# Experts' rows and results transposed on VectorE in 32x32 blocks over quarter rows, in place of TensorE transposes

## The reference

```python
def _clamped_swiglu(u):
    glu, lin = jnp.split(u, 2, axis=-1)
    glu = jnp.minimum(glu, SWIGLU_LIMIT)
    lin = jnp.clip(lin, -SWIGLU_LIMIT, SWIGLU_LIMIT)
    return glu * jax.nn.sigmoid(SWIGLU_ALPHA * glu) * (lin + 1.0)

def expert_block(args):                      # 128 tokens of one expert
    xb, e = args
    u = xb @ w_in[e] + b_in[e]               # 1024 -> 2048, the "up" product
    return _clamped_swiglu(u) @ w_out[e] + b_out[e]   # 1024 -> 1024, the "down" product

x = x + g_f[:, None] * _moe(h, ...)          # sum over a token's experts, weighted by its gates
return _rmsnorm(x, final_norm_g)
```

## Time and profile before

| | |
|---|---|
| median of 3 runs | 1981.47 us (1980.3 to 1984.21) |
| span of the profiled execution, first to last instruction | 1959.1 us |
| TensorE busy | 1923.4 us, 98% of the span |
| VectorE busy | 655.1 us, 33% |
| ScalarE busy | 467.9 us, 24% |
| GpSimd busy | 217.5 us, 11% |
| granted TensorE clock, mean | 0.997 of full speed |
| DRAM traffic, mean over the span | 265 GB/s |

### The profile page before, as it was taken

How to read it: one execution, slowest core, us unless ns; L and a number is a source line. 1 busy time by engine, 2 the same in 40 slices (tenths; PEclk the granted TensorE clock), 3 DMA queues, 4 the chain that set the end, 5 groups by cost and what they waited for, 6 DMA issues and landing times.

```text
span 1959.1 us, 50916 instructions
## 1 busy us (share of the span) xinstructions
PE 1923.4 (98%) x22971; PEld 1732.3 (88%) x22971; DVE 655.1 (33%) x1890; ACT 467.9 (24%) x1382; POOL 217.5 (11%) x250
## 2 busy tenths in 40 slices
PE   7999999999999999999999999999999999999997
PEld 4756765566999999999999999999999999999997
DVE  2655766665331212121222222222222222222224
ACT  3104544441121111111111112121211111122213
POOL 2003000001010101020201011101011110110002
PEclk9999999999999999999999999999999999999999
DMA  9880121116988888887969796969697988999986
GB/s 360 307 181 20 44 76 54 44 54 207 363 316 295 292 323 311 298 309 278 333 255 354 263 355 252 371 245 369 245 380 253 370 319 327 340 330 337 323 320 223
DMA packets 150208, 523.95 MB, mean 267 GB/s; under 512 B 10027, under 2 KB 15811, under 8 KB 149987
## 3 DMA queue, kind: packets, MB, share of 16 engines
q1 hardware_dynamic: 131186, 467.68, 65.7%
q0 software_dynamic: 17200, 52.59, 7.9%
q10 hardware_dynamic: 1600, 0.36, 0.1%
HBM read 485.34 MB, written 34.21 MB: 265 GB/s over the span
## 4 chain that ended last, share of the span: by engine, by line
PE 94%; DVE 2%; SPq 1%; DMA 1%; issue 1%; ACT 0%; POOL 0%; ACTq 0%; DVEq 0%; POOLq 0%
PE ps L1683 47%; PE ps L1721 24%; PE ps L1518 5%; PE ps L1466 4%; PE ps L1526 3%; PE ps L1671 2%; PE ps L1644 2%; PE ps L1444 2%; PE ps L1498 1%; PE ps L1462 1%; DMA ring<-in_w_qkv 1%; PE ps L1487 1%; SPq L416 0%; SPq L428 0%; PE ps L1415 0%
## 5 line engine op out<-in xcount | busy, mean ns | idle before, releaser
L1683 PE MATMUL ps<-U,ring 128*64 128x120 f32 (+11 forms) x13312 | 935.5, 270 | 1.7 <-issue 1.7
L1683 PEld LDWEIGHTS ps<-U,ring 128*64 128x64 f32 (+1 forms) x13312 | 923.1, 149 | 9.5 <-issue 7.9
L1721 PE MATMUL ps<-U,ring 128*64 128x120 f32 (+11 forms) x6656 | 468.4, 270 | 0.1
L1721 PEld LDWEIGHTS ps<-U,ring 128*64 128x64 f32 (+1 forms) x6656 | 461.4, 149 | 4.1 <-issue 3.4
L1253 DVE TENSOR_SCALAR U<-ps,U 128x120 f32<-128x120 f32 (+11 forms) x256 | 90.7, 354 | 1089.6 <-PE ps L1683 1089.6
L829 ACT ACTIVATE U<-U 128x120 f32<-128x120 f32 (+11 forms) x256 | 80.2, 313 | 889.7 <-DVE U L1253 889.7
L840 ACT ACTIVATE U<-ps,U,modT 128x120 f32<-128x120 f32 (+11 forms) x256 | 119.0, 465 | 286.8 <-PE ps L1721 286.7
L593 POOL DMA_INDIRECT acc_d<-U x43 | 43.2, 1005 | 849.5 <-DVE U L1245 845.8
L1518 PE MATMUL ps<-ring 128*128 128x512 f32 (+1 forms) x288 | 114.9, 552 | 0.0
L1518 PEld LDWEIGHTS ps<-ring 128*128 128x128 f32 x288 | 53.4, 190 | 54.4 <-issue 52.9
L815 ACT ACTIVATE U<-ps,modT,Af 128x120 f32<-128x120 f32 (+11 forms) x252 | 91.9, 469 | 9.2 <-PE ps L1656 9.2
(11 more groups left out here) (231 smaller groups left out, 1100.3 us busy)
## 6 DMA issues: line engine op xcount, KB each, us to landing
ring<-in_moe_w SPq DMA_DIRECT2D x191, 2048.0 KB, 11.1
U<-in_w_mod SPq DMA_DIRECT2D x8, 2048.0 KB, 12.2
ring<-in_w_mod SPq DMA_DIRECT2D x3, 2048.0 KB, 19.4
ring<-in_w_qkv SPq DMA_DIRECT2D x3, 2048.0 KB, 18.5
acc_d<-xr SPq DMA_DIRECT2D x10, 512.0 KB, 3.4
xr<-in_x SPq DMA_DIRECT2D x8, 512.0 KB, 9.5
ring<-in_w_o SPq DMA_DIRECT2D x2, 2048.0 KB, 8.6
xn_d<-U SPq DMA_DIRECT2D x8, 512.0 KB, 2.6
```

Source lines behind the costliest of these rows:

```text
L1683: last = pe.matmul(bank(j % 4)[lo:hi, s * 256:s * 256 + n], w[:, k, s, (j % 2) * P + lo:(j % 2) * P + hi], xT[:, k, 0:n], start=(k == 0), ...
L1721: last = pe.matmul(bank(m % 4)[lo:hi, 0:n], w[:, k, (m % 4) * P + lo:(m % 4) * P + hi], actT[:, k, 0:n], start=(k == 0), stop=(k == KT - 1))
```

## The change

- A row of 1024 features is treated as four **quarter rows** of 256. 32 tokens times 4 quarters fill 128 partitions, which is called a **turn**; a slot of width n takes ceil(n/32) turns (3 to 6; 143 over all slots). GpSimd gathers and scatters quarter rows of 1 KB by index tables (`xq_rows`, `yq_rows`), one indirect DMA for each turn, and gates one number for each quarter row.
- VectorE turns 32x32 blocks: a partition quarter then holds 32 features of its quarter row. `rows_turn(r + 1)` stands behind slot r's last activation, two instructions; `rows_back(r - 1)`, two instructions and one multiply-add for each turn, stands behind the evacuation of up product 3 (wide slot) or 5 (narrow), or 1 in the last slot.
- So that the blocks fit the products, the host lays out the weights, the norm's gain and the modulation in another order of features (`into_experts`, `out_of_experts`, `by_piece`). Input features are taken with a stride of 8 elements (`features`), in the router's transposes too.
- ScalarE scales the turned rows from SBUF to SBUF in place (`rows_scale`) instead of reading PSUM.
- Down products go to banks 4 to 7, so that they wait neither for an up product's evacuation nor up products for a down product's. Their eight K steps stand one behind the other as before.
- The index tables need a product and some VectorE instructions, placed in slot 0 (`places_by_row`, `places_product`, `places_by_quarter`).
- The first slot's rows and the last slot's results are still turned on TensorE.

```diff
+        def features(rows, k):
+            return rows.rearrange("p (n k) -> p k n", k=KT)[:, k]
...
         def back_behind(r):
-            return 4 if wide(r - 1) and not wide(r) else 0
+            return 0 if r == LAST_SLOT else 2 if wide(r) else 4
...
+            def gather_quarters(r):
+                for v in range(turns(r)):
+                    pool.indirect_dma_start(out=xq[:, v, :], out_offset=None, in_=xn_q,
+                                            in_offset=bass.IndirectOffsetOnAxis(ap=xq_rows[:, v, r:r + 1], axis=0))\
+                        .then_inc(s_g, 16)
...
             def scatter_sums(r):
-                for b, rows in blocks(r):
-                    pool.indirect_dma_start(out=acc_d, out_offset=bass.IndirectOffsetOnAxis(ap=sum_rows[0:rows, b, r:r + 1], axis=0),
-                                            in_=ysb[0:rows, b, :], in_offset=None).then_inc(s_sout, 16)
+                for v in range(turns(r)):
+                    pool.wait_ge(s_ye, turns_to(r) + v + 1)
+                    pool.indirect_dma_start(out=acc_q, out_offset=bass.IndirectOffsetOnAxis(ap=yq_rows[:, v, r:r + 1], axis=0),
+                                            in_=yq[:, v, :], in_offset=None).then_inc(s_sout, 16)
...
-            gather_rows(0)
+            gather_first_rows()
+            pool.wait_ge(s_iq, 1)
+            pool.wait_ge(s_xtp, FIRST_ROUNDS)
             for r in range(E):
-                pool.wait_ge(s_xtp, x_done[r + 1])
+                if r:
+                    pool.wait_ge(s_xv, 2 * r)
                 if r + 1 < E:
-                    gather_rows(r + 1)
+                    gather_quarters(r + 1)
                 if r == 0:
...
-                    pool.wait_ge(s_ye, y_done[r])
                     scatter_sums(r - 1)
                     gather_gates(r)
-                    pool.wait_ge(s_sout, gathers[r] * 16)
+                    pool.wait_ge(s_sout, turns_to(r) * 16)
                     gather_sums(r)
...
+            def rows_scale(r):
+
                 n = WIDTHS[r]
-                each = KT // x_rounds(r)
-                for k in range(q * each, (q + 1) * each):
-                    at = k % each * (512 // each)
-                    last = act.activation(xT[:, k, 0:n], bank(rows_bank(r, q))[:, at:at + n], ACT.Identity,
-                                          scale=Af[:, k:k + 1], bias=modT[:, 24 + k:25 + k])
+                for k in range(KT):
+                    if k % 4 == 0:
+                        act.wait_ge(s_xv, 2 * (r - 1) + k // 4 + 1)
+                    last = act.activation(xT[:, k, 0:n], xT[:, k, 0:n], ACT.Identity, scale=Af[:, k:k + 1], bias=modT[:, 24 + k:25 + k])
                 last.then_inc(s_xT, 1)
...
-                    for q in range(x_rounds(r + 1)):
-                        rows_evacuate(r + 1, q)
+                    rows_scale(r + 1)
+                if r:
+                    act.wait_ge(s_yt, 2 * r)
                 for m in range(8):
                     if r == E - 1 and m < TT - 3:
                         final_squares(m + 3)
                     act.wait_ge(s_mm, r * 16 + 8 + m + 1)
-                    act.activation(yT[:, m, 0:n], bank(m % 4)[:, 0:n], ACT.Identity, scale=modT[:, 40 + m:41 + m],
+                    act.activation(yT[:, m, 0:n], bank(4 + m % 4)[:, 0:n], ACT.Identity, scale=modT[:, 40 + m:41 + m],
                                    bias=biasT[:, 16 + m, r:r + 1]).then_inc(s_me, 1)
...
+            def rows_turn(r):
+
+                n = turns(r)
+                dve.wait_ge(s_g, x_gathered(r) * 16)
+                src = xq[:, 0:n, :].rearrange("p s (d c) -> p c s d", c=KT)
+                for h in range(2):
+                    half = slice(4 * h, 4 * h + 4)
+                    dve.transpose(xT[:, half, 0:32 * n].rearrange("p c (s t) -> p c s t", t=32), src[:, half]).then_inc(s_xv, 1)
+
+            def rows_back(r):
+
+                n = turns(r)
+                dst = turned[:, 0:n, :].rearrange("p s (c d) -> p s c d", c=KT)
+                src = yT[:, :, 0:32 * n].rearrange("p c (s t) -> p s c t", t=32)
+                for h in range(2):
+                    half = slice(4 * h, 4 * h + 4)
+                    dve.wait_ge(s_me, r * 8 + 4 * h + 4)
+                    dve.transpose(dst[:, :, half], src[:, :, half]).then_inc(s_yt, 1)
+                dve.wait_ge(s_yt, 2 * r + 2)
+                dve.wait_ge(s_gg, turns_to(r + 1) * 16)
+                dve.wait_ge(s_sg_in, sums_gathered(r) * 16)
+                for v in range(n):
+                    dve.scalar_tensor_tensor(out=yq[:, v, :], in0=turned[:, v, :], scalar=gates_q[:, r % 2, v:v + 1],
+                                             in1=yq[:, v, :], op0=ALU.mult, op1=ALU.add).then_inc(s_ye, 1)
...
                     if r and j == back_behind(r) + 1:
-                        rows_gate(r - 1)
-                        rows_out(r - 1, range(4))
+                        rows_back(r - 1)
+                    if r == 0 and j == 1:
+                        places_by_row()
+                    if r == 0 and j == 3:
+                        places_by_quarter()
                     if j >= 1:
                         activate(j - 1)
+                if r + 1 < E:
+                    rows_turn(r + 1)
 
             def output_places():
...
-            def rows_transpose(r, q):
-
-                if q == 0:
-                    pe.wait_ge(s_g, gathers[r + 1] * 16 - 16)
-                    if r >= 2:
-                        pe.wait_ge(s_ye, y_done[r - 1])
-                each = KT // x_rounds(r)
-                for k in range(q * each, (q + 1) * each):
-                    for b, rows in blocks(r):
-                        at = k % each * (512 // each) + b * P
-                        used = P if b else rows
-                        last = pe.transpose(bank(rows_bank(r, q))[:, at:at + used], xg[0:used, b, k * P:(k + 1) * P],
-                                            ident[0:used, 0:used])
-                last.then_inc(s_xtp, 1)
...
-            def rows_back(r, halves=(0, 1)):
-
-                pe.wait_ge(s_me, r * 8 + 4 * halves[-1] + 4)
-                if r:
-                    pe.wait_ge(s_ye, y_done[r])
-                for b, h in y_rounds(r):
-                    if h not in halves:
-                        continue
-                    rows = blocks(r)[b][1]
-                    for m in range(4 * h, 4 * h + 4):
-                        last = pe.transpose(bank((4 if b else 6) + h)[0:rows, (m % 4) * P:(m % 4 + 1) * P],
-                                            yT[:, m, b * P:b * P + rows], ident[:, :])
-                    last.then_inc(s_ytp, 1)
...
+            def places_product():
+
+                pe.wait_ge(s_plt, 4)
+                flat = rep_in.rearrange("p s v e -> p (s v e)")
+                pe.matmul(bank(7)[:, 0:8 * E], rep, flat[:, 0:8 * E], start=True, stop=True)
+                pe.matmul(bank(7)[:, 8 * E:2 * MAXT * E], rep[0:IDS - P, :], flat[0:IDS - P, 8 * E:2 * MAXT * E], start=True, stop=True)\
+                    .then_inc(s_plp, 1)
...
-                    if j >= 4:
+                    if r or j >= 4:
                         pe.wait_ge(s_je, r * 8 + j - 3)
-                    elif r:
-                        pe.wait_ge(s_me, r * 8 + j - 3)
                     for s in range(2):
                         for k in range(KT):
                             if r == 0 and j == 0 and k == 6:
                                 pe.wait_ge(s_wl[0], 32)
                             last = up_product(j, s, k)
                     last.then_inc(s_mm, 1)
-                    if r and j == back_behind(r):
-                        rows_back(r - 1)
-
-                if r + 1 < E:
-                    for q in range(x_rounds(r + 1)):
-                        rows_transpose(r + 1, q)
-                for m in range(8):
-                    if m % 4 == 0:
-                        pe.wait_ge(s_wl[4 + m // 4], loads_of(r, 4 + m // 4))
-                    if m < 4:
-                        pe.wait_ge(s_je, r * 8 + m + 5)
-                    else:
+                    if r == 0 and j == 2:
+                        places_product()
+
+                def down_product(m, k):
+                    w = piece(4 + m // 4).rearrange("p (k n) -> p k n", k=KT)
+                    for lo, hi in parts:
+                        last = pe.matmul(bank(4 + m % 4)[lo:hi, 0:n], w[:, k, (m % 4) * P + lo:(m % 4) * P + hi], actT[:, k, 0:n],
+                                         start=(k == 0), stop=(k == KT - 1))
+                    return last
+
+                pe.wait_ge(s_wl[4], loads_of(r, 4))
+                for m in range(4):
+                    if r:
                         pe.wait_ge(s_me, r * 8 + m - 3)
-                    w = piece(4 + m // 4).rearrange("p (k n) -> p k n", k=KT)
+                    elif m == 3:
+                        pe.wait_ge(s_iq, 1)
                     for k in range(KT):
                         if m == 0:
```

(10 more changed lines are left out.)

268 lines of the change are left out of this document (169 added, 99 removed).

## The result

The kernel became slower: a median of 2365.8 us (2362.2 to 2367.5, 4 runs) against 1981.6 us, a ratio of 1.193 (95% interval 1.191 to 1.195). The forecast was 1930 us, and neither its range nor a rival reached this. The page of the changed kernel: the span and the engines, the granted clock, the chain by engine, the costliest groups.

A forecast was written before the change was run, and what follows sets the result against it. The prediction took TensorE's instructions to bound the kernel. Removing 84 us and losing 16, 6.5, 3.5 and 6.3 us gave 51.7 us less than the median of 1981.5: 1930 us, range 1912 to 1948.

The forecast's parts named there:

- Costed at nothing: GpSimd's indirect DMAs, 27 of 41 us in a 120 wide slot, and other DMA work were taken to add no time.
- VectorE waiting for gathered sums: Sign in the changed profile that would show the forecast wrong: VectorE held up by sums that GpSimd gathers; no size given.
- Removed, 84 us: TensorE's 680 transposes at 119 ns, 81 us, plus 3 us for switches between products and transposes, would go.
- (1): Down product 0 waits for the activations, about 0.51 us in each of 31 slots: 16 us lost.
- (2): VectorE late through `rows_back` in 88 and 104 wide slots behind wide ones: 6.5 us lost.
- The rivals of twice and three times the rate: VectorE's block transposes cost twice an ordinary instruction (1967 us, chance 0.13) or three times (2015 us, chance 0.05).
- (3): ScalarE late evacuating down product 0, behind strided `rows_turn` and scalings, in 88 and 104 wide slots: 3.5 us lost.
- 0.31 us in place of 0.47: ScalarE's time for each scaling of rows, expected to fall by reading SBUF.
- (4): Once-only costs: slot 0's tables 1.3 us, strided weight loads 2 us, last slot 3 us; 6.3 us lost.
- 22.4 us around it: Time outside the profiled span, taken to stay unchanged between the span of 1907 us and the median of 1930 us.
- DMA becomes the bound: Rival: many 1 KB packets make the DMA engines the limit in the last slots; 1940 to 1975 us, chance 0.09.

The follow-up runs named there:

- experiment 2: The kernel before with 12 more indirect gathers by GpSimd in every slot from 1 on, read by nobody: 2499.6 us, ratio 1.260.
- experiment 4: The changed kernel with GpSimd waiting for TensorE's products between its indirect DMAs: 1969.4 us, ratio 0.993.
- experiment 8: The changed kernel without its gathers of gates (all gates 0.25, output not the layer's): 2132.0 us, ratio 1.077.
- experiment 1: The changed kernel with GpSimd moving whole rows, 172 indirect DMAs in the loop in place of 568 (output not the layer's): 1935.9 us, ratio 0.977.
- the last version: The changed kernel, indirect DMAs paced to one or two per product, results turned earlier in narrow slots behind narrow ones: 1930.4 us, ratio 0.975.
- experiment 7: The kernel before with 12 more small DMAs, issued by SyncE, in every slot from 1 on: 1983.7 us, ratio 1.002.
- the paced version: The changed kernel with GpSimd's indirect DMAs held apart by waits for TensorE's products; successive pacings measured 1969.4, 1936.2 and 1930.4 us.

## Why the prediction was wrong

**The step that failed** is the one under "Costed at nothing": "GpSimd: a round of a 120 wide slot is 16 indirect DMAs x 1.28 = 20.5 us ... 27 of 41 us", covered because nobody waits for its sums. Its sizes were right: in a train the DMAs came 1.25 us apart in the median, and in the loop no engine waited for a gathered row. What was wrong is to count them only as time of GpSimd. By experiments 2, 4 and 8 a long train of indirect DMAs is time in which TensorE gets on only by a few matmuls: in a narrow slot all of it but the first 2 to 3 us, in a wide one what follows the first 10 to 13 us. The slower products behind the stalls come on top: 256 + 181 us. The kernel before never has more than 4 such DMAs one behind the other, mostly two or three, and in the shown profile TensorE does not stop for them, so its trace could not give the price; I should have bounded it, since their number went from 175 to 554 (lines 593, 581, 587 and 575 before; 646, 628, 639 and 617 now). The sign that was to show the step wrong, "VectorE waiting for gathered sums", looks only for a late result.

**Removed, 84 us: right for the pair of slots that it was read from.** The chain of experiment 1 through slots 24 and 25:

```profile
1589.00 26.31 PE ps L1792 x480
...
1617.05 12.68 PE ps L1816 x226
...
1629.84 26.56 PE ps L1792 x511
...
1658.09 12.08 PE ps L1816 x227
1670.17 0.05 PE ps L1792
```

The first row starts 32 matmuls, 1.75 us, into slot 24, so the pair is 1670.2 - 1589.0 + 1.75 = 83.0 us, against 85.92 and a forecast of 81.88 + 2 x 0.51 = 82.9. The other slots were not compared one by one.

**(1) Down product 0 waits for activations, 16 us: the wait was right, its sum with (2) was too low.** The 0.51 us of the earlier trace rows are waits of weight loads, and so they are compared with weight loads. In experiment 1 these wait 0.16 + 0.33 us in slot 24 and 0.20 + 0.31 in slot 25, as forecast. In all they wait 27.7 us for line 1380 in the loop, where (1) and (2) gave 22.5. Some 12.5 us of this are six narrow slots behind wide ones, 112 and 120 wide, with 1.1 to 2.4 us each, where no lateness was forecast; there the short stalls behind three indirect DMAs stand, told of in experiment 1. The row shown in experiment 1 has 15.5 us for the matmuls' own wait. That this is near 16 is luck: 11 of them are these same six slots.

**(2) VectorE in `rows_back`: the durations were right.** Groups of the changed kernel by form, turned in (line 1327), turned back (1337):

```profile
L1327 DVE STREAM_TRANSPOSE U<-U 128x512 f32<-128x512 f32 x34 | 35.6, 1086 | 0.0
...
L1337 DVE STREAM_TRANSPOSE xr<-U 128x512 f32<-128x512 f32 x32 | 20.7, 685 | 0.0
...
L1327 DVE STREAM_TRANSPOSE U<-U 128x768 f32<-128x768 f32 x10 | 15.0, 1537 | 0.0
...
L1337 DVE STREAM_TRANSPOSE xr<-U 128x768 f32<-128x768 f32 x12 | 11.0, 952 | 0.0
```

0.69 and 0.95 us had been taken for 512 and 768 elements, 1.5 for the strided 768, and 0.40 for a sum of 256, which takes 0.42 (1.68 us for four in a row). What VectorE's lateness alone cost, forecast as 6.5 us, was not measured apart from (1). The rivals of twice and three times the rate were wrong by this.

**(3) ScalarE late, 3.5 us: right in experiment 1** (2.7 us for the down products' evacuation), 12.5 us in the last version, which turns results at another place. That ScalarE gains elsewhere, "0.31 us in place of 0.47", was wrong: a scaling of the turned rows takes 0.47 us at 120 wide.

**(4)** Of its parts only the router's strided weight loads can be read: 189 ns in the changed kernel where they took 141, 1.34 times and not 1.58. The others were not measured apart.

**The profiled time was not the median's.** I took 1907 us for the span and 22.4 us around it. Experiment 1 has a span of 1931.6 us in a launch of 1933.3, so 1.7 us around it, and a median of 1935.9. Its down products are busy 26 us longer than the earlier trace rows's kernel had them (494.5 against 468.4). The kernel before seems to lose such time too in other executions: with the small DMAs of experiment 7, which change its time by 0.2%, the down products take 479.3 us and wait 7.6 in a span of 1981.5 us, in the one shown 468.4 and 0.1. So the shown execution was lighter than the median by some 20 us, and most of the difference lies in the loop, not around it. The two errors cancel in 1930 us. What tests the sum is the saving between medians: 46.7 us in experiment 1 and 48.5 in the last version, against 51.7. That the last version's median is 1930 to the us is luck, since it moves DMAs and VectorE's work about in ways that the sum knew nothing of.

**Order and DMA.** The rival "DMA becomes the bound" is out: the paced version moves the same packets in 1933 us and no weight is waited for.
